# Early start of TensorE, earlier casts and decays, and the output weight in four pieces, in one encoder layer

## What is computed

```python
h = rmsnorm(x, attn_norm_g)
z = h @ w_in
na_q, na_k, na_v, hg_q, hg_ff, hg_fb, hg_i, hg_g, mem_q = jnp.split(z, offsets, axis=-1)
na_out = neighbourhood_attention(na_q, na_k, na_v, na_rpb)
o = hgrn2_bidirectional(hg_q, hg_i, hg_ff, hg_fb, lb_fwd, lb_bwd)   # S_t = diag(f_t) S_{t-1} + k_t v_t, o_t = S_t^T q_t
hg_out = _rms_normalize(o) * hg_out_norm_g * silu(hg_g)
mem_out = memory_cross_attention(mem_q, rmsnorm(mem, mem_norm_g), w_mem_kv)
x = x + jnp.concatenate([na_out, hg_out, mem_out], axis=-1) @ w_out
h2 = rmsnorm(x, ffn_norm_g)
x = x + peer_ffn(h2, peer_w_query, peer_sub_keys, peer_u, peer_v)
return rmsnorm(x, final_norm_g)
```

## Time and profile before

| | us |
|---|---|
| median of three runs | 1747.9 |
| the profiled execution, its own time | 1744.18 |
| its span | 1742.3 |
| PE busy in the span | 1685.8 |
| DVE / POOL / ACT busy | 1128.6 / 859.9 / 771.4 |
| end of the first block, start of the second (PE) | 213.5 |

### The profile page before, as it was taken

How to read it: one execution, slowest core, us unless ns; L and a number is a source line. 1 busy time by engine, 2 the same in 40 slices (tenths; PEclk the granted TensorE clock), 3 DMA queues, 4 the chain that set the end, 5 groups by cost and what they waited for, 6 DMA issues and landing times. The chain is left out here.

```text
span 1742.3 us, 30626 instructions
## 1 busy us (share of the span) xinstructions
PE 1685.8 (97%) x10448; PEld 1363.0 (78%) x10448; DVE 1128.6 (65%) x2446; ACT 771.4 (44%) x1261; POOL 859.9 (49%) x711
## 2 busy tenths in 40 slices
PE   6999999999999999999989999999999999999997
PEld 5877645589999989999977777777777777777774
DVE  3776755447878868888356566566566665665665
ACT  5354455543334455555444344344344344344343
POOL 2374230067787750000047566666566666566663
PEclk9999999999999999999999999999999999999999
DMA  5321250154554455677789999999999999999996
GB/s 184 108 77 58 64 179 1 63 195 162 173 173 148 155 188 180 240 257 253 275 279 356 325 358 337 327 362 330 336 353 326 335 361 331 329 363 334 332 352 243
DMA packets 170627, 426.87 MB, mean 245 GB/s; under 512 B 24241, under 2 KB 75569, under 8 KB 170417
## 3 DMA queue, kind: packets, MB, share of 16 engines
q1 hardware_dynamic: 119584, 272.87, 46.4%
q0 software_dynamic: 45056, 134.38, 20.1%
q10 hardware_dynamic: 5904, 18.56, 2.7%
HBM read 389.69 MB, written 36.04 MB: 244 GB/s over the span
## 5 line engine op out<-in xcount | busy, mean ns | idle before, releaser
L2127 PE MATMUL psum<-h2hi,u_hi 128*128 128x512 f32 x1016 | 365.1, 398 | 0.0
L1944 POOL DMA_INDIRECT rows<-in_peer_v,row_i x248 | 243.7, 983 | 218.6 <-PE psum L2161 152.8
L1923 POOL DMA_INDIRECT spot<-acts_first,spot_i x256 | 276.9, 1082 | 83.4 <-issue 78.6
L2128 PE MATMUL psum<-h2hi,u_lo 128*128 128x256 f32 x1024 | 286.7, 280 | 0.0
L2127 PEld LDWEIGHTS psum<-h2hi,u_hi 128*128 128x128 f32 x1016 | 190.6, 188 | 69.3 <-issue 25.1
L1972 ACT ACTIVATE gel<-pre 128x256 f32<-128x256 f32 x128 | 53.4, 417 | 406.2 <-DVE pre L2017 406.2
L2139 PE MATMUL psum<-v_hi,w_hi 128*128 128x512 f32 x512 | 203.3, 397 | 2.3 <-DVE w_lo L2030 2.3
L2007 DVE TENSOR_TENSOR u_lo<-u_raw,u_hi 128x1024 fp32r<-128x1024 f32 x126 | 154.4, 1226 | 76.8 <-ACT u_hi L1962 76.8
L2139 PE MATMUL psum<-v_hi,w_lo 128*128 128x512 f32 x512 | 203.5, 397 | 0.0
L2139 PE MATMUL psum<-v_lo,w_hi 128*128 128x512 f32 x512 | 203.2, 397 | 0.0
L2128 PEld LDWEIGHTS psum<-h2hi,u_lo 128*128 128x128 f32 x1024 | 193.4, 189 | 4.4
(11 more groups left out here) (284 smaller groups left out, 4080.4 us busy)
## 6 DMA issues: line engine op xcount, KB each, us to landing
u_raw<-in_peer_u SPq DMA_DIRECT2D x256, 512.0 KB, 4.2
v_raw<-in_peer_v SPq DMA_DIRECT2D x128, 512.0 KB, 6.8
acts_first<-gel SPq DMA_DIRECT2D x128, 128.0 KB, 2.5
gates<-chunk ACTq DMA_DIRECT2D x32, 512.0 KB, 2.7
g_in<-gates SPq DMA_DIRECT2D x64, 256.0 KB, 8.5
wring<-in_w_in SPq DMA_DIRECT2D x24, 512.0 KB, 3.5
wq_raw<-in_w_query SPq DMA_DIRECT2D x16, 512.0 KB, 5.2
w_out<-in_w_out SPq DMA_DIRECT2D x1, 4096.0 KB, 14.0
```

Source lines behind the costliest of these rows:

```text
L1923: pool.indirect_dma_start(spot[:, t:t + 1], None, spots, bass.IndirectOffsetOnAxis(ap=spot_i[:, t:t + 1], axis=0)).then_inc(s_spot, 16)
L1944: pool.indirect_dma_start(rows[:, slot, :], None, values, bass.IndirectOffsetOnAxis(ap=row_i[:, t:t + 1], axis=0)).then_inc(s_rows[q % PER ...
L2127: pe.matmul(bank, u_hi[:, s % 2, k, :], h2hi[:, k, :], start=(k == 0), stop=False)
L2128: last = pe.matmul(bank[:, 0:DENSE], u_lo[:, s % 2, k, :], h2hi[:, k, GATHERED:T], start=False, stop=(k == KD - 1))
```

## The change

There are four edits.

1. ACT issues the identity first, alone on `s_const`, and PE waits for it alone. The other three small loads raise `s_late`, on which ACT and DVE now wait in the old places. The counts of later waits on `s_late` are raised by three loads.
2. ACT casts the two halves of the second projection's weight right after the casts of h, ahead of the squares of the memory; the walk of the jobs leaves them out at job ("e", 0, 0).
3. On DVE `prepare(decays, ...)` stands ahead of the evacuation of the level's first bank instead of behind it.
4. SP loads the output weight in four transfers, one per piece and in the order of the pieces, then the gain, then the four tiles of x. PE waits for the first transfer before the first piece, and for the other three and the gain before the second.

```diff
-        consts = [(ident[:], "ident"), (gain_a[:], "attn_norm_g"), (gain_m[:], "mem_norm_g"),
-                  (bound[:], "hg_lower_bound")]
+        consts = [(gain_a[:], "attn_norm_g"), (gain_m[:], "mem_norm_g"), (bound[:], "hg_lower_bound")]
...
         @block.scalar
         def _(act):
+            act.dma_start(ident[:], dram["ident"]).then_inc(s_const, 16)
             for dst, name in consts:
-                act.dma_start(dst, dram[name]).then_inc(s_const, 16)
+                act.dma_start(dst, dram[name]).then_inc(s_late, 16)
...
-            act.wait_ge(s_const, 16 * len(consts))
+            act.wait_ge(s_late, 16 * len(consts))
...
+            split_next(split_w, jobs[at[("e", 0, 0)]])
             act.wait_ge(s_mem, 16 * MT)
...
-                split_next(split_w, job)
+                if n > len(early_jobs):
+                    split_next(split_w, job)
...
-            dve.wait_ge(s_const, 16 * len(consts))
+            dve.wait_ge(s_late, 16 * len(consts))
...
+                if job[0] == "lev" and job[2] % 2 == 0:
+                    prepare(decays, job[2] // 2, job[1])
                 if job[3] == "dve":
                     empty(job[:3])
...
                 if job[0] == "lev" and job[2] % 2 == 0:
                     hp, lv = job[2] // 2, job[1]
-                    prepare(decays, hp, lv)
                     if lv + 1 == INTER_AT:
                         inter_decays(hp)
...
-            pe.wait_ge(s_const, 16 * len(consts))
+            pe.wait_ge(s_const, 16)
...
         @block.sync
         def _(sp):
+            for pair in PIECES:
+                ks = slice(pair[0], pair[1] + 1)
+                sp.dma_start(w_out[:, ks, :], dram["w_out"].rearrange("(k p) n -> p k n", p=P)[:, ks, :]) \
+                    .then_inc(s_wo if pair == PIECES[0] else s_in, 16)
+            sp.dma_start(gain[:], dram["ffn_norm_g"]).then_inc(s_in, 16)
             for n in range(NT):
                 sp.dma_start(x_sb[:, n, :], columns_of(dram["x"], n)).then_inc(s_x, 16)
-                if n == 0:
-                    sp.dma_start(gain[:], dram["ffn_norm_g"]).then_inc(s_in, 16)
-                    sp.dma_start(w_out[:], dram["w_out"].rearrange("(k p) n -> p k n", p=P)).then_inc(s_wo, 16)
...
+                if piece and t == 0:
+                    pe.wait_ge(s_in, 16 * len(PIECES))
```

More of the change, by code:

```diff
@@ L603, in empty @@
                     if lv == 0 and h == 0:
-                        dve.wait_ge(s_late, 16 * len(late_consts))
+                        dve.wait_ge(s_late, 16 * (len(consts) + len(late_consts)))
                     mask = masks[:, lv, :].unsqueeze(1).to_broadcast([P, NT, P])
@@ L794, in run @@
                     pe.wait_ge(s_osq, a + 1)
-                    pe.wait_ge(s_late, 16 * len(late_consts))
+                    pe.wait_ge(s_late, 16 * (len(consts) + len(late_consts)))
                     last = pe.matmul(out, halves[:], osq[:, a, :], start=True, stop=True)
@@ L1054, in _ @@
                 if c == PAIRS + TURN_AT + 1:
-                    act.wait_ge(s_in, 16)
+                    act.wait_ge(s_in, 16 * len(PIECES))
                 if c == STEPS + 1:
```

## The result

The changed kernel took 1734.24 us (median of six runs, 1730.82 to 1736.09), the kernel before 1747.17 us in the same comparison. The ratio is 0.9927, 95% interval 0.9914 to 0.9940. The profiled execution took 1736.09 us for a span of 1734.2, so it is the longest of the six.

A forecast was written before the change was run, and what follows sets the result against it. PE, busy 97% of the span, was taken to bound the kernel, so gains are its gaps and slow stretches: 1.7 + 6.4 + 3.1 + 2.2 = 13.4 us, from 1747.9 to 1734.5 us, range 1730 to 1742.

The forecast's parts named there:

- (2): Levels: moved decays collide with POOL's products, so the decays' term becomes a loss of 2.9 us; 1740.5 us, chance 0.16.
- (3): Third projection: PE arrives 8 us earlier, finds casts or weights late, and the 6.4 us go; 1741 us, chance 0.08.
- The start: Program start: PE waits for the identity alone, so the first projection begins and ends 1.7 us earlier; bounds 1.2 and 1.83.
- The casts: Second projection: the 4.23 us gap goes and the clock stays up behind it, 2.2 us more; together 6.4 us.
- The decays: Levels: decays ahead of evacuations come 1 to 2 us earlier and cut PE's 4.6 us of waits by 3.1 us.
- under 2 us of waits: Levels: sign that the forecast holds, PE's waits there adding up to less than 2 us.
- The second case of the prediction: Levels: decays and POOL's products hamper each other, POOL late by 1.43 us per block at two levels; loss 2.9, chance 0.16.
- its strict reading: Levels: moved blocks that begin during POOL's products cost POOL 1.4 us each, leaving the decays' term about 1.5 us.
- The output weight: First output projection: the first quarter lands before PE needs it, so the 2.27 us wait goes; 2.2 us, bounds 0 and 2.3.
- PE gets there at 226.65: First output projection: PE reaches the first piece at 226.65 us, after the first weight quarter lands near 219.
- DVE's first sum: After the output projection: sign that DVE's first sum comes some 13 us earlier than 252.6 us.

The follow-up runs named there:

- the second execution: The changed kernel with all four edits, run and profiled once more against the kernel before: 1735.17 us, ratio 0.9940.
- the opening unfilled: Without the 16 idle PE transposes that a follow-up added to the changed kernel in the second block's opening; with them 1731.77 us, ratio 0.9918 to the kernel before.

## Why the prediction was right, step by step

The forecast was 13.4 us; the medians differ by 12.9, and in the comparison in which the changed kernel was run again by 11.6. No run of the changed kernel came near the 1740.5 and 1741 of rivals (2) and (3), and PE did not wait at the third projection. By the landmarks:

- **The start** (1.7): 1.1 in the profile after, 1.8 alone, 2.4 in the second execution. The term was right as a mean: over the six executions with only the new start the first projection begins at 13.8 on average, over the four with the old one at 15.6. The bounds (1.2 to 1.83) were too narrow, as they took only one later moment of the quick pace into account.
- **The casts** (6.4): 6.7 by the stretch to the memory's transposes (17.7 to 11.0). Gap and slow stretch went together. The next pair of casts began at 24.06, where 23.7 was forecast, and PE did not wait.
- **The decays** (3.1): 1.9 to 2.2. This is the step that was mis-sized. Of the waits 2.8 us are left (2.5 in the second execution), not 1.5, and the sign "under 2 us of waits" did not come. The forecast took POOL's waits to fall by 2.2 of 2.9; those for the products fell to 1.0 (0.3 in the second execution), but a new one of 0.9 for the cross queries, which the prediction did not price, took the place of what was won. The second case of the prediction named DVE's decays and POOL's products side by side, and priced it too high (a loss of 2.9): in the step shown above DVE loses more by it than POOL. The median of POOL's product rose from 1.30 to 1.48 us, which agrees with the rule on the shared port in the Trainium skill, "SBUF — State Buffer", section "Who interferes with whom"; its strict reading gave 1.5 us, the measured 2 lies between.
- **The output weight** (2.2): 2.3 alone, 0.5 in the profile after, -0.4 in the second execution. The wait went as forecast, and no new one came. What failed is "PE gets there at 226.65", 13.1 us into the block: it does so only if the clock stays up, and with all four edits and the opening unfilled it did in none of three executions. In the kernel with the decays alone the old wait hid such a fall. DVE's first sum came 10.3 us earlier (242.3), not some 13.

The sum of the steps with the clock up is 1.8 + 6.7 + 2.1 + 2.3 = 12.9. That it equals the difference of the medians is luck as far as the profiles go: in both profiled executions of the changed kernel the clock fell, and 10.2 and 10.9 us were won at the end of the output projection. So the forecast was right by the start and the casts, 8.1 us of it; the rest was too high by about 1 us in the decays, and in the output weight by as much as the clock took.

The 2.1 us lost behind that are not shown to be the change's. From there to the end, where all the kernels are alike, the thirteen profiled executions took from 1407.5 to 1412.4 us. The other kernels with all four edits lie between 1407.7 and 1411.0, but the two executions of the changed kernel itself are the two longest (1412.4 and 1412.1). Most of the differences arise in two stretches, 590 to 650 and 840 to 900 us. There PE's waits differ from execution to execution, and the clock falls at other moments: from 590 to 610 us it was 0.91 after, and 1.00 at the same work before (600 to 620). A single profiled pair (1744.18 to 1736.09, 8.1 us) would have told a wrong size.

## What to carry to other kernels

A wait can hide another loss: before it is priced, look at what else runs slow under it, here PE's clock. Where an engine stands idle for reasons of order, a few casts moved ahead of work that is needed later can be worth the gap and the slow stretch behind it, 6.7 us here. Compare landmarks of stages over several executions, since one profile mixes the change with what differs from run to run.

## What was not expected of the hardware

PE's quick pace at the start of the program comes at another moment in each execution: 24 transposes begun at 7.2 to 7.3 us took 4.27, 4.85 and 5.36 us. The Trainium skill, "TensorE: Matmul & The Clock Gate", Part 1, says that the count of slow matmuls at a start varies from run to run, and the traces agree. And the clock of a kernel that keeps PE busy for 97% of its span fell to 1.2 GHz in an opening where PE worked 0.6 to 0.9 of 2 us, in five executions and not in three with the same gaps of PE, at a cost of 1.8 to 2.7 us where nothing hid it.
